# Delta rule's scan on Trainium2: products with 128 weight columns written as two halves of 64, two zero quadrants left out

## The reference, cut to what matters

```python
w, u = solve(eye - a, concat(kb * exp(gcum), v * beta))      # a: strictly lower triangular
v_new = u - w @ s                                            # the products old and new
attn = (q @ k.T) * exp(where(lower, diff, -inf))             # the product queries
o = (q * exp(gcum)) @ s + attn @ v_new                       # both parts of state's second half
s_new = exp(g_last) * s + (k * exp(g_last - gcum)).T @ v_new
```

## Time and profile before

| | us |
|---|---|
| median of three runs | 4213.47 (4212.18 to 4232.05) |
| the profiled execution | 4199.34 |
| its span in the trace | 4197.5 |
| PE busy | 3847.4 (92%), 19086 matmul records |
| DVE busy | 1757.3 (42%) |
| ACT busy | 955.7 (23%) |
| POOL busy | 677.9 (16%) |
| mean granted clock of TensorE | 0.948 |

### The profile page before, as it was taken

One profiled execution on the slowest core, in us unless ns is written; L12 is line 12 of the kernel. 1 busy time (PEld: TensorE's weight loads), 2 busy tenths in 40 slices (PEclk: granted clock), 3 DMA queues, 4 the chain that ended last, 5 costly groups with the idle time before them and its releaser, 6 DMA issues.

```text
span 4197.5 us, 47909 instructions
## 1 busy us (share of the span) xinstructions
PE 3847.4 (92%) x19086; PEld 2426.4 (58%) x19086; DVE 1757.3 (42%) x3797; ACT 955.7 (23%) x1833; POOL 677.9 (16%) x653
## 2 busy tenths in 40 slices
PE   5897997988999999999998997899899998899899
PEld 3467884666457444444443577876554557775554
DVE  2585563235444133333333725521361453621441
ACT  4123331222100210000005202311351311220441
POOL 3002340022000122222214102211001101211001
PEclk7998897998999999999999999999999999999899
DMA  5301112035346101111111202220100412211101
GB/s 182 113 14 27 26 26 89 26 121 175 103 161 212 41 30 50 40 41 50 40 44 57 106 21 81 71 64 31 46 1 25 156 31 66 76 54 47 39 26 40
DMA packets 215403, 277.79 MB, mean 66 GB/s; under 512 B 24301, under 2 KB 174024, under 8 KB 214288
## 3 DMA queue, kind: packets, MB, share of 16 engines
q1 hardware_dynamic: 201904, 206.17, 16.0%
q0 software_dynamic: 13280, 68.57, 4.3%
HBM read 239.89 MB, written 34.81 MB: 65 GB/s over the span
## 4 chain that ended last, share of the span: by engine, by line
PE 83%; DVE 8%; issue 3%; ACT 3%; DMA 2%; POOL 1%; SPq 0%; POOLq 0%; DVEq 0%; ACTq 0%
PE ps L2776 17%; PE ps L808 16%; PE ps L2647 8%; PE ps L830 7%; PE ps L3606 6%; PE ps L3880 4%; PE ps L2408 3%; PE ps L4089 2%; DMA big<-hs_scratch 1%; PE ps L2844 1%; PE ps L854 1%; PE ps L4072 1%; DVE big L3701 1%; PE ps L4057 1%; PE ps L1451 1%
## 5 line engine op out<-in xcount | busy, mean ns | idle before, releaser
L2776 PE MATMUL ps<-big 128*128 128x512 f32 x1624 | 697.1, 592 | 0.0
L808 PE MATMUL ps<-big 128*128 128x512 f32 (+1 forms) x1760 | 685.1, 550 | 2.9 <-DMA big<-hs_scratch 2.9
L808 PEld LDWEIGHTS ps<-big 128*128 128x128 f32 x1760 | 335.5, 192 | 343.5 <-issue 334.2
L2776 PEld LDWEIGHTS ps<-big 128*128 128x128 f32 x1624 | 308.6, 190 | 388.4 <-issue 385.3
L2647 PE MATMUL ps<-big 128*128 128x512 f32 (+1 forms) x896 | 359.3, 562 | 3.0 <-DVE big L4207 2.0
L830 PE MATMUL ps<-big 128*128 128x256 f32 (+1 forms) x1792 | 318.4, 341 | 10.2 <-DVE big L1898 10.2
L830 PEld LDWEIGHTS ps<-big 128*128 128x128 f32 x1792 | 288.1, 194 | 39.5 <-DVE big L1898 10.3
L2647 PEld LDWEIGHTS ps<-big 128*128 128x128 f32 x896 | 169.6, 190 | 187.6 <-issue 180.8
L2969 DVE SCALAR_TENSOR_TENSOR big<-ps,big 128x512 f32<-128x512 f32 x212 | 159.0, 750 | 242.9 <-PE ps L2776 208.9
L3606 PE MATMUL ps<-big 128*128 128x256 f32 x1152 | 251.8, 380 | 7.1 <-DMA big<-hs_scratch 3.9
L3606 PEld LDWEIGHTS ps<-big 128*128 128x128 f32 x1152 | 217.6, 190 | 37.4 <-issue 6.7
(11 more groups left out here) (474 smaller groups left out, 5374.8 us busy)
## 6 DMA issues: line engine op xcount, KB each, us to landing
big<-in_w_mlp SPq DMA_DIRECT2D x32, 1024.0 KB, 5.4
big<-in_w_in SPq DMA_DIRECT2D x29, 1024.0 KB, 5.3
big<-in_w_mod SPq DMA_DIRECT2D x24, 1024.0 KB, 5.3
big<-in_w_ada SPq DMA_DIRECT2D x24, 1024.0 KB, 6.5
big<-us_scratch SPq DMA_DIRECT2D x72, 256.0 KB, 4.3
hs_scratch<-big POOLq DMA_DIRECT2D x3, 5120.0 KB, 15.8
big<-c_dft SPq DMA_DIRECT2D x12, 1024.0 KB, 5.5
xs_scratch<-big POOLq DMA_DIRECT2D x16, 640.0 KB, 3.7
```

The source lines that it names most:

```text
L808: t = e.matmul(b[:, 0:n], wv[:, k, 128 * m:128 * m + 128], K.hT[:, k, t0:t0 + n], start=(k == 0), stop=(k == 7))
L2776: t = e.matmul(z, w[:, k, c], y, start=(first and k == 0), stop=(k == nk - 1), skip_group_check=not first)
```

## The change

Every product of 128 weight columns in `queries`, `old`, `new` and the output part of `state` is written as two products of 64 weight columns, the halves in turn (`self.halves`), each to its own 64 partitions of the same bank. In `new` and in the A part of the output, the product for the half J takes only the 64 contraction rows of J, since the rows of I are zero there, and so isn't given the zero quadrant; the product for I keeps all 128 rows. The memsets of these quadrants go. The product of 96 weight columns (L1506) stays, and so do all waits, all signals and the order of steps.

```diff
@@ queries
+        k4, q4 = m.kT[:, :, ts], m.qT[:, :, ts]
         for h in range(4):
-            t = e.matmul(b[:, 128 * h:128 * h + 128], m.kT[:, h, ts], m.qT[:, h, ts], start=True, stop=True)
+            for p in self.halves:
+                t = e.matmul(b[p, 128 * h:128 * h + 128], k4[:, h, p], q4[:, h, :], start=True, stop=True)
@@ old
+        k4 = m.kT[:, :, ts]
         for h in range(4):
-            t = e.matmul(b[:, 96 * h:96 * h + 96], m.kT[:, h, ts], m.S[d][:, 96 * h:96 * h + 96], start=True, stop=True)
+            for p in self.halves:
+                t = e.matmul(b[p, 96 * h:96 * h + 96], k4[:, h, p], m.S[d][:, 96 * h:96 * h + 96], start=True, stop=True)
@@ new
         for h in range(4):
-            t = e.matmul(b[:, 96 * h:96 * h + 96], ch["XF"][:, 128 * h:128 * h + 128], ch["vn"][:, 96 * h:96 * h + 96],
-                         start=True, stop=True)
+            for p in self.halves:
+                k = self.J if p is self.J else slice(0, 128)
+                t = e.matmul(b[p, 96 * h:96 * h + 96], h4(ch["XF"], 128)[k, h, p], ch["vn"][k, 96 * h:96 * h + 96],
+                             start=True, stop=True)
@@ state
             for h in range(4):
-                o = b[:, 96 * h:96 * h + 96]
-                e.matmul(o, ch["A"][:, 128 * h:128 * h + 128], vn[:, 96 * h:96 * h + 96], start=True, stop=False)
-                t = e.matmul(o, ch["qe"][:, 128 * h:128 * h + 128], S[:, 96 * h:96 * h + 96], start=False, stop=True)
+                sl = slice(96 * h, 96 * h + 96)
+                for p in self.halves:
+                    k = self.J if p is self.J else slice(0, 128)
+                    e.matmul(b[p, sl], h4(ch["A"], 128)[k, h, p], vn[k, sl], start=True, stop=False)
+                for p in self.halves:
+                    t = e.matmul(b[p, sl], h4(ch["qe"], 128)[:, h, p], S[:, sl], start=False, stop=True)
@@ GdnVector.__init__
-        for x in (self.ch["XF"], self.ch["A"]):
-            e.memset(h4(x, 128)[self.I, :, self.J], 0.0).then_inc(self.V.sem, self.V.up())
```

## The result

| | before | after |
|---|---|---|
| median, us | 4212.83 (4187.80 to 4232.05, 4 runs) | 4258.93 (4247.03 to 4265.45, 4 runs) |
| profiled execution, us | 4199.34 | 4247.03 |
| its span | 4197.5 | 4245.2 |
| the scan's stage in it, first record to last instruction | 339.8 to 664.4: 324.6 | 339.5 to 711.2: 371.7 |
| everything ahead of the stage, and behind it | 339.8, 3533.1 | 339.5, 3534.0 |

The kernel is slower: the ratio of the times is 1.0128, with an interval of 1.0097 to 1.0159. Against a forecast of 4257.5 us in a range of 4232 to 4300 the median is 4258.9. Nearly the whole difference lies in the stage that was changed: 47.1 of 47.7 us between the two profiled executions.

What follows compares the result with a forecast made beforehand. PE's queue was taken to set the pace, with some 24 us idle. `new` +24.4, output +20.7, `old` -5.1, `queries` -1.1 gave +39, half clock +5: +44 on 4213.5, so 4257.5 us, range 4232 to 4300.

Steps and rivals of the forecast that it cites:

- The price of a change of shape: In `new` and output, switching 64-row and 128-row weights costs 0.133 us to the second record, 0.172 to the next shape.
- the price of halves by turns in one shape: In `old`, a pair of both halves with 96 moving columns takes 0.082 us, between bounds of 0.059 and 0.109.
- What is added reaches the end: The output's added PE time reaches the kernel's end wholly, and that of `new` too; +1.3 and +1.22 us a step.
- DVE's wait at the state's update: DVE's wait for the output product at L1647 goes up from 44 us by about 20.
- Rival B: PE's idle time in the scan's stage takes in the growth, 24 us at the most: 4234 us; chance 0.13.
- Rival A: In `new` and output, 64-row and 128-row shapes in different column halves run by turns: -17 us, 4197; chance 0.08.
- -5.1 for `old`: `old`, in one shape by turns, takes 0.96 us against 1.21, 20 times; half of the saving may be lost.
- -1.1 for `queries`: `queries`, 8 pairs at 0.109 us and a shorter first record, saves 0.07 us, 16 times.
- PE's idle time is all the room there is: In the scan's stage PE's queue sets the pace, with some 24 us of idle time as the only room.
- rival C: The clock falls more often in the changed stage: 4284 us for another 100 us at half clock, 4318 whole; chance 0.22.
- The +5 for the steps at half clock: Some four steps each of `new` and output lie at half clock, adding 1.97 and 1.9 us: +5 us.
- 24.4 and 20.7: Growth in us at full clock: `new` +1.22 for each of 20 steps, output +1.3 for each of 16.

Runs made afterwards that it cites:

- all-rows kernel: The whole change, but products for J keep all 128 contraction rows and the memsets stay; 4174.78 us against 4206.33 for the kernel before, repeated at 4178.21 against 4209.21.
- the two dear parts alone: Two kernels, each the kernel before with one part changed: only `new` (4244.09 us, ratio 1.0069) or only the output (4229.53 us, ratio 1.0042).
- `old` without turns: Kernel before with `queries` and `old` changed, but `old` takes four products for one half, then four for the other; 4196.31 us, ratio 0.9974 to the kernel before.
- grouped kernel: The whole change, but `new` runs its four products for J, then its four for I; 4231.46 us, ratio 1.0061 to the kernel before.

## Why the prediction was right, and where two errors cancelled

**The price of a change of shape: right.** The term was 0.133 to the second record and 0.172 to the next shape, between bounds of 0.107 and 0.187, and of 0.15 and 0.205. For a step entered from a 64 x 64 neighbour, as the one shown, 0.080 and seven times 0.133 and 0.172 each make 2.22 us from the first start of `new` to its last; measured 2.50 - 0.25 = 2.25. The output was worked out as 4 x 0.77 = 3.08; measured 3.13. The all-rows kernel confirms the price of halves by turns in one shape: 0.133 + 6 x 0.082 + 0.007 + 0.172 = 0.80 for `new`, measured 0.82; 1.46 for the output, measured 1.49.

**What is added reaches the end: right.** 1.22 and 1.3 us for a step gave 7.3 and 7.8 for six places; measured 7.27 and 8.6. DVE's wait at the state's update was to grow by about 20 and grew by 21.7. The stage was to go from 328 to some 372, counted from 336; so counted it ends at 711.2 and takes 375.2, 47 more for the forecast's 44. (The 371.7 in the first table starts at the stage's first record; that it equals 372 is chance.) Rival B (idle time takes the growth in) fell: PE's idle time in six places went from 6.2 to 5.8.

**Rival A fell.** It had the 64-row and the 128-row half side by side. The records of the all-rows kernel are what A would have been, and they are the faster ones. A's arithmetic for what such records take stands (0.80 and 1.46 above), though not its -17 for the kernel, of which 8 arrived at equal clock. Its premise for this kernel was false. The second statement of the page "TensorEngine Tiling (Array Packing)" of the Trainium skill (Key Properties), that changing the tiling mode drains the engine, is the one that decides here. The trace agrees in so far as the next shape is held back by 0.172 us where the same shape follows after 0.082, and it adds that 64 x 64 next to 128 x 64 is such a change; that the engine is emptied no run here shows, since a record is drawn 0.25 us long and the next shape starts earlier. Its first statement, that tiles work in parallel, the traces bear out within one shape only: a pair of halves takes 0.082 us together.

**What is saved doesn't reach the end: wrong.** The step that failed is the sum's -5.1 for `old` and -1.1 for `queries`, of which at least 3.6 was to arrive. `old` did fall on PE, from 1.06 us to the next line (532.70 to 533.76 below) to 0.82 (L1488 above). But the kernel with these two alone takes 80.73 for 80.89 in six places, where the sum had 6 x 0.32 = 1.9 less, and -0.4 at equal clock. One place in the trace shows why. First the kernel before, then the one with `old` and `queries` changed:

```profile
532.70 1.13 PE L1484 MATMUL ps<-big 96*128 96x96 f32 x8
...
533.76 1.75 PE L1451 MATMUL ps<-big 64*64 64x64 f32 x48
...
534.23 0.45 DVE L1621 STREAM_TRANSPOSE big<-big 128x256 f32<-128x256 f32 x1
534.60 0.95 DVE L1639 SCALAR_TENSOR_TENSOR big<-ps,big 128x96 f32<-128x96 f32 x4
...
535.70 1.10 PE L1495 MATMUL ps<-big 128*128 128x96 f32 x8 [0.19 <-DVE big L1639]
```

```profile
536.98 0.88 PE L1488 MATMUL ps<-big 96*64 96x96 f32 x16
...
537.80 1.99 PE L1451 MATMUL ps<-big 64*64 64x64 f32 x48
...
538.52 0.45 DVE L1625 STREAM_TRANSPOSE big<-big 128x256 f32<-128x256 f32 x1
538.89 0.95 DVE L1643 SCALAR_TENSOR_TENSOR big<-ps,big 128x96 f32<-128x96 f32 x4
...
539.98 1.10 PE L1499 MATMUL ps<-big 128*128 128x96 f32 x8 [0.19 <-DVE big L1643]
```

The step of DVE that follows `old` starts 1.90 us behind the start of `old` in the one and 1.91 in the other, because DVE's queue is full of the other chains' transposes until then; `new` starts 3.00 behind it in both. PE doesn't even show the gain as idle time. Its 48 records of L1451 start 0.24 earlier and last 0.24 longer, 1.99 for 1.75, and end 2.81 behind the start of `old` in both. The whole 3.00 us in the two kernels (PE, PEld, DVE, ACT, POOL busy):

```profile
532.70:535.70 3.00, 2.81 (x61) 2.58 (x57) 2.90 (x11) 0.93 (x3) 2.46 (x4) 1.00 0.00 0
```

```profile
536.98:539.98 3.00, 2.81 (x68) 2.42 (x65) 2.90 (x13) 0.92 (x3) 2.53 (x4) 1.00 0.00 0
```

DVE is busy for 2.90 of them in both: in this stretch DVE sets the pace, and PE's busy time of 2.81 hides gaps between records, since one record is drawn 0.22 us long and the next usually starts after far less. So the prediction's reading that PE's idle time is all the room there is was wrong too. In the six places the same is seen in sum: PE's busy time falls by only 0.4 (74.74 to 74.34) and its idle time grows by 0.2. That DVE rarely waited was in the trace of before: it waited for `old` 5 times in 20, 3.9 us in all. I had said that half might be lost; nearly all is.

**Half clock: wrong by a factor of two.** I compared 53.2 us for three places with three times 15.8 and took 0.19 us lost for each us at half clock. But places aren't all 15.8 apart: the six at full clock average 80.89 / 6 = 13.5. From the seventh `new` to the eleventh the kernel before, with 30.7 us of it at half clock, takes 69.26 us, and the kernel with `old` and `queries` changed, which does the same at full clock, 57.03:

```profile
466.44:535.70 69.26, 65.92 (x993) 62.02 (x993) 39.15 (x113) 24.00 (x65) 25.10 (x34) 0.78 0.10 25
```

```profile
482.95:539.98 57.03, 52.51 (x1056) 48.25 (x1057) 37.83 (x114) 24.04 (x65) 25.10 (x34) 1.00 0.12 31
```

That is 12.2 us for 30.7, or 0.40 for each. The 64 runs say the same: 0.001 of the mean clock is 4200 x 0.001 / 0.5 = 8.4 us at half clock and costs 3.1 us, 0.37 for each. So rival C would have cost twice what I gave it. It didn't come about: the four executions of the kernel after have a mean clock of 0.9435, the 64 of the kernel before 0.945. The +5 for the steps at half clock can't be told apart in the total: the two dear parts alone have 3.4 and 1.9 us more at equal clock than their sums of 24.4 and 20.7, which would fit it, but the whole change has no such surplus.

The growth without any saving is 24.4 + 20.7 = 45.1; +44.7 at equal clock and +46 between the medians were measured. The forecast's +44 came from 45.1 - 6.2 + 5: the lost saving and the term for the half clock had opposite signs and about the same size. The result was closer than the working deserved.

**A version that beats both.** Halves by turns with 128 rows for J, the fourth and eighth kernel, take 4174.8 and 4178.2 us against 4206.3 and 4209.2 for the kernel before: ratios 0.9908 and 0.9943. Of these 31 us the six places explain part: 77.71 for 80.89, 3.2 us, where the sum for PE has 6 x 0.9 = 5.4, so that here too some of what PE saves doesn't arrive; that DVE's queue takes it here as well is likely and wasn't looked at place by place. Over 20 places that is some 8 to 11 us, as the comparison at equal clock has it (-8). The rest of the 31, some 20 us, goes with the clock: the 18 runs of these two have 0.949 to 0.955, those of before 0.937 to 0.953. In its profile the stage takes 299.0 us at a mean clock of 0.93, against 324.6 at 0.87:

```profile
339.40:638.40 299.00, 252.85 (x5568) 230.14 (x5568) 194.59 (x567) 112.26 (x304) 122.62 (x159) 0.93 0.11 28
```

```profile
339.80:664.40 324.60, 282.56 (x4864) 263.43 (x4864) 194.88 (x567) 112.28 (x304) 122.40 (x159) 0.87 0.10 26
```

By these rows the stage has about 42 us at half clock for 84. At 0.40 each that is 17 us, which with 3.2 / 6 x 20 = 11 makes 28, and the stage is 25.6 shorter. The eighth kernel repeated this (0.949 to 0.955, 77.71), so it is hardly chance; why the clock falls less often in this kernel stays open. No experiment changed the clock alone.

## What to carry to other kernels

Before splitting matmuls, write down the shape of weights (up to 64 rows or more, up to 64 columns or more) of each record in the order in which they run: here each change of that shape added about 0.2 us ((2.44 - 0.82) / 7 in `new`, (3.13 - 1.49) / 8 in the output), and a step that alternated between shapes took two to three times as long as one that multiplied by zeros. In this kernel work that was added to PE arrived in full, while work that was taken away arrived only where nothing else stood in the queue of the engine that waits for it. That is read from how often that engine really waited (here 5 times in 20) and from its own busy time in the stretch (2.90 of 3.00 us), not from PE's busy share. Where runs of one kernel differ by more than the effect, compare a stretch at one granted clock, from one and the same step to another, in both traces.

## What the runs showed of the hardware that I had not expected

- Two column halves weren't served in strict order. In `old` without turns, eight records of the first half stand ahead of the second half's in the program, and yet the trace has a second series of records that begins beside the fifth (starts 5 ns apart; 1.20 us for the step instead of over 1.3). Read as the second half, which nothing in a record names, it began some four records ahead of its turn.
- The same program spans 1.2% from run to run (4182 to 4235 us), and its mean granted clock, from 0.937 to 0.953, goes with all but 4 us of it (the standard deviation around the line). In the profiles the time outside the scan's stage moves little, 3527 to 3538 us behind it, while the stage itself had between 41 and 145 us at half clock.
- A multiplication by 64 more rows, all zero, cost nothing: with 96 moving columns the 64 x 64 records of the grouped kernel follow each other after some 0.086 us (0.104 for the second, 0.083 for the rest), and a pair of halves of 128 x 64 or 96 x 64 takes 0.082 (L1501 of the all-rows kernel, L1488).
